# Three units in each of five gate column groups computed as seven block products

## What is computed

```python
h = rms_norm(x, norm_mix)
(qa, ka, va, qb, kb, vb, qc, ..., gc, gates) = split_cols(h @ w_in)   # gates: 3 * 2048 columns
y_a, y_b, y_c = swa_attention(...), stick_breaking(...), nsa_attention(...)
g_a, g_b, g_c = split(gates, 3)
merged = sigmoid(g_a) * (y_a @ w_br_a) + sigmoid(g_b) * (y_b @ w_br_b) + sigmoid(g_c) * (y_c @ w_br_c)
x = x + merged @ w_out
h = rms_norm(x, norm_ffn)
x = x + (silu(h @ w_gate) * (h @ w_up)) @ w_down
return rms_norm(x, norm_final)
```

## Time and profile before

| | us |
|---|---|
| time, median of 3 runs (1356.83 to 1357.32) | 1356.87 |
| time of the profiled execution | 1354.56 |
| its span | 1352.8 |
| of it PE busy | 1343.6 |
| DVE busy | 1016.8 |
| ACT busy | 729.9 |
| POOL busy | 46.6 |

### The profile page before, as it was taken

The page is one execution under the profiler, slowest core; times in us unless marked ns, Lnnn a source line. Parts: engine busy times, 40 slices in busy tenths (PEclk is TensorE's granted clock), DMA queues, the critical chain, the costliest instruction groups (busy, mean ns, idle before and its releaser), DMA issues.

```text
span 1352.8 us, 26568 instructions
## 1 busy us (share of the span) xinstructions
PE 1343.6 (99%) x11202; PEld 1308.9 (97%) x11202; DVE 1016.8 (75%) x1380; ACT 729.9 (54%) x958; POOL 46.6 (3%) x70
## 2 busy tenths in 40 slices
PE   9999999999999999999999999999999999999997
PEld 8888999999999999999999999999999999999997
DVE  6454557667644766767899999889897899988984
ACT  7333356656545664456655555555454555555554
POOL 4000000000000110000000000000000000000003
PEclk9999999999999999999999999999999999999999
DMA  7767555444565667555566666665666666666563
GB/s 261 249 224 222 182 171 157 152 141 141 156 187 171 188 195 229 185 188 168 184 208 204 213 195 192 195 203 181 210 211 202 194 215 191 193 196 232 191 204 139
DMA packets 135265, 261.08 MB, mean 193 GB/s; under 512 B 8448, under 2 KB 25408, under 8 KB 134768
## 3 DMA queue, kind: packets, MB, share of 16 engines
q1 hardware_dynamic: 132944, 251.14, 58.3%
q0 software_dynamic: 1792, 7.57, 1.6%
q10 hardware_dynamic: 416, 0.75, 0.2%
HBM read 257.33 MB, written 2.10 MB: 192 GB/s over the span
## 4 chain that ended last, share of the span: by engine, by line
PE 99%; DMA 0%; ACT 0%; DVE 0%; issue 0%; DVEq 0%
PE bank L686 22%; PE bank L688 22%; PE bank L687 22%; PE bank L928 9%; PE bank L925 9%; PE bank L927 9%; PE bank L674 3%; PE bank L824 1%; PE bank L735 1%; DMA x<-in_x 0%; PE bank L784 0%; PE bank L1071 0%; PE bank L736 0%; PE bank L872 0%; PE bank L850 0%; PE bank L864 0%
## 5 line engine op out<-in xcount | busy, mean ns | idle before, releaser
L1412 DVE TENSOR_TENSOR weight_lo_ring<-raw_ring,weight_hi_ring 128x1024 fp32r<-128x1024 f32 (+2 forms) x479 | 580.5, 1216 | 242.3 <-ACT weight_hi_ring L1134 185.6
L1134 ACT ACTIVATE weight_hi_ring<-raw_ring 128x1024 fp32r<-128x1024 f32 (+2 forms) x431 | 449.8, 1049 | 421.6 <-PE bank L688 206.2
L686 PE MATMUL bank<-weight_hi_ring,hT_hi 128*128 128x256 f32 (+2 forms) x1276 | 380.9, 298 | 0.0
L687 PE MATMUL bank<-weight_lo_ring,hT_hi 128*128 128x256 f32 (+2 forms) x1276 | 375.5, 294 | 0.0
L688 PE MATMUL bank<-weight_hi_ring,hT_lo 128*128 128x256 f32 (+2 forms) x1276 | 375.5, 294 | 0.0
L686 PEld LDWEIGHTS bank<-weight_hi_ring,hT_hi 128*128 128x128 f32 x1276 | 239.8, 188 | 10.0 <-issue 3.4
L687 PEld LDWEIGHTS bank<-weight_lo_ring,hT_hi 128*128 128x128 f32 x1276 | 239.9, 188 | 6.1
L688 PEld LDWEIGHTS bank<-weight_hi_ring,hT_lo 128*128 128x128 f32 x1276 | 239.7, 188 | 6.3
L686 PE MATMUL bank<-weight_hi_ring,h2T_hi 128*128 128x256 f32 x704 | 195.2, 277 | 0.0
L687 PE MATMUL bank<-weight_lo_ring,h2T_hi 128*128 128x256 f32 x704 | 194.4, 276 | 0.0
L688 PE MATMUL bank<-weight_hi_ring,h2T_lo 128*128 128x256 f32 x704 | 194.4, 276 | 0.0
(11 more groups left out here) (292 smaller groups left out, 2457.7 us busy)
## 6 DMA issues: line engine op xcount, KB each, us to landing
raw_ring<-in_w_in SPq DMA_DIRECT2D x96, 512.0 KB, 3.4
raw_ring<-in_w_gate SPq DMA_DIRECT2D x88, 512.0 KB, 4.3
raw_ring<-in_w_up SPq DMA_DIRECT2D x88, 512.0 KB, 4.0
raw_ring<-in_w_down SPq DMA_DIRECT2D x88, 512.0 KB, 4.4
raw_ring<-in_w_in SPq DMA_DIRECT2D x55, 480.0 KB, 4.3
raw_ring<-in_w_out SPq DMA_DIRECT2D x32, 512.0 KB, 3.9
raw_ring<-in_w_br_c SPq DMA_DIRECT2D x16, 256.0 KB, 3.9
raw_ring<-in_w_br_a SPq DMA_DIRECT2D x16, 256.0 KB, 7.2
```

Source lines behind the costliest of these rows:

```text
L686: pe.matmul(dst, x_hi, w_hi, start=opening, stop=False, skip_group_check=True)
L687: pe.matmul(dst, x_hi, w_lo, start=False, stop=False, skip_group_check=True)
L1134: act.activation(whi[:, s, :, 0:width(u)], raw[:, s, :, 0:width(u)], ACT.Copy)\
L1412: dve.tensor_tensor(lo, w, hi.bitcast(F32), ALU.subtract).then_inc(lo_ready, 1)
```

## The change

In gate groups 7 to 11, units 1, 3 and 5 of the eight are done in seven block products: 15 units. For that

- DVE makes sums of the left operand's blocks (`hT`) for the three units once, at slots 55, 57 and 59, in front of the branch evacuation where the slot has one, and their low parts one slot later; ACT writes the high parts;
- each of the 15 units has the three weight sums and their low part on DVE and their high part on ACT, as in the feed-forward stages;
- the spare bank pair is the one that the branch before the gate has used. So at the gate's unit 1 PE waits until that branch is emptied. After unit 5 ACT copies one of the two banks to `sig`, DVE folds both into the quarters of `sig` (three operations), and PE waits for this before the next branch;
- at the gate's end DVE adds the two main banks to `sig` (two operations) in place of ACT's sigmoid; ACT takes the sigmoid in place two slots later.

New buffers lie over parts of `proj` that are no longer read. The core of the diff:

```diff
+GATE_SEVEN = (1, 3, 5)
+GATES_BY_SEVENS = (7, 8, 9, 10, 11)
+GATE_SUMS_SLOT = 55
...
+GATE_MID = {u + GATE_SEVEN[-1]: q for q, (_, _, u, _) in enumerate(CHUNKS) if gate_by_sevens(q)}
+GATE_SUM_AT = {U_MIX + GATE_SUMS_SLOT + 2 * n: n for n in range(len(GATE_SEVEN))}
...
 def evac_engine(q):
 
-    return "act" if CHUNKS[q][0] == "gate" else "dve"
+    return "act" if CHUNKS[q][0] == "gate" and not gate_by_sevens(q) else "dve"
...
+            def gate_unit(u, lhs, q, j):
+
+                pe.wait_ge(lo_ready, u + 1)
+                sums = None
+                if is_seven(u):
+                    n = GATE_SEVEN.index(j)
+                    if gates_folded(q) == 1:
+                        pe.wait_ge(hT_sum_lo, n + 1)
+                    if n == 0:
+                        pe.wait_ge(emptied[evac_engine(q - 1)], evac_count(q - 1))
+                    sums = (hS[n][:, 0, :, :], hS[n][:, 1, :, :])
+                pair, other = 2 * (q % 2), 2 * (1 - q % 2)
+                block_unit(u, ("gate", q), lhs, UK * j, sums, pair, pair + 1, j == UPC - 1, six=other).then_inc(unit_used, 1)
...
                 if j == 0:
                     pair_free(q)
+                    if gate_by_sevens(q - 1):
+                        pe.wait_ge(gate_folded, gates_folded(q - 1))
...
+            def copy_gate_products(v, q):
...
+                act.wait_ge(unit_used, v + 1)
+                act.wait_ge(emptied["dve"], evac_count(branch_q[i - SIG]))
+                quarter = sig[:, i % SIG, :, :].rearrange("p t (c n) -> p (t c) n", c=2)
+                act.activation(quarter[:, 0:4:3, :], bank[2 * (1 - q % 2)][:, :].rearrange("p (q c) -> p q c", q=2),
+                               ACT.Copy).then_inc(gate_copied, 1)
...
+                if v in GATE_MID:
+                    copy_gate_products(v, GATE_MID[v])
+                if v - 1 in GATE_SUM_AT:
+                    m = GATE_SUM_AT[v - 1]
+                    act.wait_ge(hT_summed, m + 1)
+                    act.activation(hS[m][:, 0, :, :], h_total[m][:, :, :], ACT.Copy).then_inc(hT_sum_hi, 1)
+                if v - 2 in CHUNK_OF:
+                    p, jp = CHUNK_OF[v - 2]
+                    if gate_by_sevens(p) and jp == UPC - 1:
+                        act.wait_ge(emptied["dve"], evac_count(p))
+                        for t in range(TT):
+                            tile = sig[:, CHUNKS[p][1] % SIG, t, :]
+                            last = act.activation(tile, tile, ACT.Sigmoid, scale=rstd[:, t:t + 1])
+                        last.then_inc(emptied["act"], 1)
...
+            def sums_of_hT(n):
+
+                k0 = UK * GATE_SEVEN[n]
+                chain(dve.tensor_tensor(h_both[:, :, :], hT_hi[:, k0:k0 + 2, :].bitcast(F32),
+                                        hT_lo[:, k0:k0 + 2, :].bitcast(F32), ALU.add))
+                (h11, h12), (h21, h22) = ((h_both[:, k, 0:P], h_both[:, k, P:S]) for k in range(UK))
+                s1, s2, s3, s4 = (h_total[n][:, r, :] for r in range(4))
+                dve.tensor_tensor(s3, h12, h11, ALU.subtract)
+                chain(dve.tensor_tensor(s1, h12, h22, ALU.add))
+                chain(dve.tensor_tensor(s2, s1, h11, ALU.subtract))
+                dve.tensor_tensor(s4, h21, s2, ALU.subtract).then_inc(hT_summed, 1)
...
+            def fold_gate(v, q):
...
+                dve.wait_ge(unit_used, v + 1)
+                dve.wait_ge(gate_copied, gates_folded(q))
+                chain(dve.tensor_tensor(gate_u_two[:, :], quarter[:, 0, :], quarter[:, 3, :], ALU.add))
+                chain(dve.tensor_tensor(quarter[:, 1:3, :], seven, gate_u_two[:, :].unsqueeze(1).to_broadcast([P, 2, Q4]),
+                                        ALU.add))
+                dve.tensor_tensor(quarter[:, 3, :], seven[:, 0, :], quarter[:, 2, :], ALU.add).then_inc(gate_folded, 1)
+
+            def finish_gate(v, q):
...
+                dve.wait_ge(unit_used, v + 1)
+                dve.wait_ge(gate_folded, gates_folded(q))
+                dve.tensor_tensor(quarter[:, 1:3, :], two, quarter[:, 1:3, :], ALU.add)
+                dve.tensor_tensor(quarter[:, 0:4:3, :], three, quarter[:, 0:4:3, :], ALU.add).then_inc(emptied["dve"], 1)
...
+                if v in GATE_SUM_AT:
+                    sums_of_hT(GATE_SUM_AT[v])
+                if v - 1 in GATE_SUM_AT:
+                    lo_of_hT_sums(GATE_SUM_AT[v - 1])
+                if v in GATE_MID:
+                    fold_gate(v, GATE_MID[v])
+                if j == n - 1 and gate_by_sevens(q):
+                    finish_gate(v, q)
                 if j == n - 1 and kind == "branch":
                     s, c = i // NC_D, i % NC_D
                     dve.wait_ge(unit_used, v + 1)
-                    dve.wait_ge(emptied["act"], evac_count(gate_q[i]))
+                    dve.wait_ge(emptied["act"], i + 1)
```

More of the change, by code:

```diff
@@ L128, with gate_by_sevens @@
 LAST_BANK = 6
+CHUNK_OF = {}
+for _q, (_k, _i, _u, _n) in enumerate(CHUNKS):
+    for _j in range(_n):
+        CHUNK_OF[_u + _j] = (_q, _j)
+def gate_by_sevens(q):
+    return q < Q_FFN and CHUNKS[q][0] == "gate" and CHUNKS[q][1] in GATES_BY_SEVENS
 def by_sevens(h, c):
@@ L141, in is_seven @@
 def is_seven(u):
+    if U_MIX <= u < U_OUT:
+        q, j = CHUNK_OF[u]
+        return gate_by_sevens(q) and j in GATE_SEVEN
     if not U_FFN <= u < U_END:
@@ L226, in evac_engine, with gates_folded @@
 def evac_engine(q):
-    return "act" if CHUNKS[q][0] == "gate" else "dve"
+    return "act" if CHUNKS[q][0] == "gate" and not gate_by_sevens(q) else "dve"
+def gates_folded(q):
+    return sum(gate_by_sevens(p) for p in range(q + 1))
 def evac_count(q):
@@ new lines, in quarters, with block_unit, block, total @@
+            def quarters(u, k, c):
+                return tuple(m[:, u % RING, k, c * Q4:(c + 1) * Q4] for m in (whi, wlo))
+            def block_unit(u, key, lhs, k0, sums, two, three, stop, six=6):
+                def block(k, t):
+                    return tuple(m[:, k0 + k, t * P:(t + 1) * P] for m in lhs)
+                if not is_seven(u):
+                    for k in range(UK):
+                        into(key, three, 0, block(k, 0), quarters(u, k, 0), stop)
+                        into(key, two, 0, block(k, 0), quarters(u, k, 1), stop)
+                        into(key, two, 1, block(k, 1), quarters(u, k, 0), stop)
+                        m = into(key, three, 1, block(k, 1), quarters(u, k, 1), stop)
+                    return m
+                def total(r):
+                    return tuple(m[:, r, :] for m in sums)
+                def extra(r):
+                    return tuple(m[:, r, :] for m in ext_buffer(u))
+                into(key, six, 0, block(0, 0), quarters(u, 0, 0), True)
+                into(key, three, 0, block(1, 0), quarters(u, 1, 0), stop)
+                into(key, two, 0, total(3), quarters(u, 1, 1), stop)
+                into(key, six, 1, total(1), quarters(u, 0, 1), True)
+                pe.wait_ge(ext_ready, N_SEVEN[u] + 1)
+                into(key, six + 1, 0, total(0), extra(0), True)
+                into(key, six + 1, 1, total(2), extra(1), True)
+                return into(key, two, 1, block(1, 1), extra(2), stop)
@@ L916, in act_transposes @@
                             m.then_inc(aT_full, 1)
[L918 to L961, removed]
             def up_unit(u, i, j):
@@ new lines, in finish_gate @@
+            def finish_gate(v, q):
+                quarter = gate_quarters(q)
+                two, three = (bank[2 * (q % 2) + b][:, :].rearrange("p (q c) -> p q c", q=2) for b in range(2))
+                dve.wait_ge(unit_used, v + 1)
+                dve.wait_ge(gate_folded, gates_folded(q))
+                dve.tensor_tensor(quarter[:, 1:3, :], two, quarter[:, 1:3, :], ALU.add)
+                dve.tensor_tensor(quarter[:, 0:4:3, :], three, quarter[:, 0:4:3, :], ALU.add).then_inc(emptied["dve"], 1)
```

69 lines of the change are left out of this document (55 added, 14 removed).

## The result

The changed kernel takes 1370.24 us (median of 6 runs, 1366.14 to 1374.21) against 1356.85 for the kernel before on the same chip (6 runs): ratio 1.0103, 95% interval 1.008 to 1.0125. It is slower by about 13.4 us; 1365.4 was forecast. A ratio is taken over all runs and can differ from the quotient of two medians by up to 0.0008.

The account below looks back on a forecast made before the run. PE was taken to bound the kernel, busy 99% of the span. Waits of 13.6 us less 5.1 of saved matmuls give +8.5, so 1356.9 becomes 1365.4 us; range 1358 to 1371.5.

Parts of the forecast that it names:

- last sign: The forecast is wrong if DVE reaches the branch evacuations on time, or if the clock falls after slot 101.
- likeliest case: PE waits at slots 61, 81, 91, 101 and 108 outweigh the saved matmuls: +8.5 us, 1365.4 us; chance 0.60.
- rival C: PE standing still may lose its clock, one unit then costing another 2.7 us: 1368 to 1371 us; chance 0.13.
- Saved matmuls: Mixing stage: 15 units lose 3 matmuls each, 45 x 0.113 = 5.1 us off PE.
- The waits: PE waits at each gate's unit 1 for the branch evacuation: 2.7, 0, 2.9, 1.7, 4.5 us at slots 61 to 101.
- The stretch beside POOL's mask: Before slot 81, DVE's weight sums take longer while POOL's mask runs: 0.7 us taken, between 0 and 0.73.
- ACT's chain freed of the sigmoid: Before slot 81, ACT's Abs, Exp, Ln (4.1 us) no longer stand behind the sigmoid.
- Slot 108: Weights queued behind the x reload delay the fold to 20.6 us against PE's 18.8: wait 1.8, bounds 0 and 3.5.
- rival A: The lead absorbs DVE's added work, as in the up product: the waits vanish, 1351.8 us remains; chance 0.11.
- Rival B: Only the waits at slots 61 and 81 come, the later ones half: net +3.5, 1360.4 us; chance 0.16.

Follow-up runs that it names:

- the work alone: The changed kernel with all added DVE and ACT work, but PE does eight products everywhere and doesn't wait for the branch evacuation at unit 1: 1363.89 us, ratio 1.0062.

## Why the prediction was right, and where it was off

The direction and the mechanism of the waits held; the size came out 4.8 us low, inside the range. That it stayed inside owes something to luck: a wait of 1.8 that was forecast did not come, and 6.3 us that were not in the sum did, 4.3 of clock and 2.0 of slower pace. By the prediction's own last sign (wrong if the clock falls after slot 101) its likeliest case failed, and rival C, given 0.13, is what happened.

- *Saved matmuls*, -5.1: the page has 11157 matmuls instead of 11202, 45 fewer. Right.
- *The waits.* Forecast 2.7, 0, 2.9, 1.7, 4.5 for slots 61, 71, 81, 91, 101; measured 2.61, 0, 2.36, 2.17, 4.36. Right to within 0.6 us each, 11.8 against 11.5 together. It came from laying DVE's and ACT's written order out in durations from rows, event by event, and not from shares of busy time.
- *The stretch beside POOL's mask*, 0.7: 0.70 (1.39 - 0.69). By the rule of the Trainium skill (SBUF — State Buffer, "Who interferes with whom") any such operation of DVE meets the lock, not the split alone; the row above agrees.
- *ACT's chain freed of the sigmoid*, at slot 81: right, shown by the kernel with groups 9 to 11.
- *Slot 108*, forecast 1.8, measured none. The arithmetic of the fold was right: the timeline has it ended at 531.06, 20.5 after PE left the wait of slot 101 (510.58), forecast 20.6. What failed is PE's own arrival, forecast at 18.8. The clock fall behind slot 101 cost PE 2.8, so it came at 21.5 (532.07), behind the fold. With units 3 and 5, where there is no fall, the wait is there.
- *The clock*, put into rival C at 0.13. It came on top of the forecast's waits, +4.3 in the profile: this is the term that was mis-sized, at zero. C priced one more unit after one or two waits, 2.7 each, and gave 1368 to 1371; the median lies in that. The rule of the Trainium skill that an idle TensorE goes back to its lower level (TensorE: Matmul & The Clock Gate, "Part 1") is borne out by the rows at 510 to 516. After these runs C would deserve most of the chance: all seven waits longer than 3 us were followed by a fall.
- *The slower pace*, +2.0: not foreseen, and its cause stays open. Another 0.6 us of the 13.3 is assigned to nothing.
- *The lead absorbs the work* (rival A): ruled out for the change, and by the work alone also for the work without its wait, where 3.1 us of waits for low parts remain.
- *Signs and sums*: DVE over 85% was forecast for the stretch of the stick-breaking heads; in 425 to 525 it is busy 84%. Rival B halves the later waits, 1.7, 4.5 and 1.8, to 3.0; half of them is 4.0, which makes B 1361.4. The forecast doesn't hang on it.

The explanation was weaker. The forecast read the waits as a matter of one unit's distance, and the two edits that only gave more distance or a better order recovered at most 2.4 us. What recovered the time was to ask two units later with a quarter less work, and to free slot 108's weights. How the 13.3 us divide between the wait and the work is not shown. The wait without work costs 5 us, the work without that wait 9.1, but some 5 of the 9.1 stand at slot 108, where the changed kernel waits for nothing, and a PE that is faster by 5.1 us asks earlier. The work alone was not run with the early reload, which could tell the two costs apart.

## What to carry to other kernels

Where several engines follow a written order, spare share says little: lay out each engine's order up to the event that PE will ask for, in durations from rows, and compare it with PE's arrival. Before a buffer is lent to a second use, look when it comes free now: here one wait without any work cost 5 us. Price a PE wait at more than its length, because the clock may fall behind it, and look what the next wait does when the first one delays PE. If moving the wait only moves the idle time, take work away rather than reorder it.

## What the runs showed of the hardware

- *The clock after a wait.* Over the profiles of the changed kernel and of nine of the experiments, all seven waits of PE longer than 3 us (3.22 to 6.05) were followed by a granted clock of 0.50, and seven of the twelve between 1.9 and 2.8 us; none shorter than that. The same 2.61 us wait at slot 61 was followed by it in the kernel with groups 7 and 8 and in the changed kernel with the early reload, and not in the changed kernel. At 0.50 matmuls start 0.213 us apart instead of 0.113, and most falls cost 1.4 to 2.8 us.
- *Two paces at full clock.* Of two stretches of the same work at granted clock 1.00, one runs at 0.1133 us per matmul (335 in 38 us, the window of before) and the other at 0.1178 (323 in 38 us, the changed kernel). The slower pace lasts 30 to 40 us in several kernels (518.7 to 550.5 with units 3 and 5, 400.5 to 439 with units 2, 4 and 6), and 74 us at the end of two profiles. In these it starts and ends only where PE's series was broken, by a wait, by another step or by a pause of as little as 0.1 us (at 412.8 with groups 7 and 8); it stands in short stretches of the kernel before too. One and the same place, the end, has the one pace in some executions and the other in others. No experiment took it apart.
- *A 2 MB reload delays small loads behind it.* Issued at its old place it made ACT wait 6.96 us for slot 108's weights, issued one mask earlier 2.29 us, with the same kernel otherwise. From issue to landing the branch loads of 485 to 535 took 8.8 us and 5.0 us (medians of eight).
